# Differential attention between the last tiles of its value product and the first of its output product, with its norms on GpSimd

## The reference, cut to what matters

```python
q = rms_norm(z[..., :1024].reshape(bsz, seq, 8, 2, 64), q_gain)
k = rms_norm(z[..., 1024:2048].reshape(bsz, seq, 8, 2, 64), k_gain)
v = z[..., 2048:].reshape(bsz, seq, 8, 128)
# for each block of 128 queries, 8 heads, 2 halves c of a head:
logits = einsum('bqhcd,bkhcd->bhcqk', q_blk, k) / 8
p = softmax(logits - slope[h] * dist)
attn = p[:, :, 0] - lam * p[:, :, 1]
o = einsum('bhqk,bkhe->bqhe', attn, v)
# after all blocks
o = rms_norm(o, out_gain) * (1.0 - lambda_init)      # over the 128 of a head
x = x + o.reshape(bsz, seq, 1024) @ diff_w_out
```

## Time and profile before

| | us |
|---|---|
| median of 3 executions (1834.36 to 1842.99) | 1838.56 |
| the profiled execution | 1837.14 |
| its span, first to last instruction | 1835.3 |
| TensorE busy | 1746.8 (95%) |
| VectorE, ScalarE, GpSimd busy | 972.2, 766.4, 131.1 |

### The profile page before, as it was taken

The page is one execution under the profiler, slowest core; times in us unless marked ns, Lnnn a source line. Parts: engine busy times, 40 slices in busy tenths (PEclk is TensorE's granted clock), DMA queues, the critical chain, the costliest instruction groups (busy, mean ns, idle before and its releaser), DMA issues.

```text
span 1835.3 us, 32123 instructions
## 1 busy us (share of the span) xinstructions
PE 1746.8 (95%) x14193; PEld 1436.9 (78%) x14193; DVE 972.2 (53%) x1353; ACT 766.4 (42%) x1180; POOL 131.1 (7%) x99
## 2 busy tenths in 40 slices
PE   6998889889999999999999998989999999999999
PEld 5877778778887788888887886558888788888887
DVE  5477656436343465535644345984524355633652
ACT  4243444425553344313433234873654244422430
POOL 1001221230010000000000022010010000000000
PEclk9999999999999999999999999999999999999999
DMA  7210000124331232222222222003322223222321
GB/s 242 81 46 2 4 4 18 48 105 149 114 115 46 73 110 94 92 92 92 92 93 91 95 89 69 1 1 115 115 92 69 92 89 95 92 92 92 92 96 66
DMA packets 96454, 149.42 MB, mean 81 GB/s; under 512 B 3479, under 2 KB 50170, under 8 KB 96314
## 3 DMA queue, kind: packets, MB, share of 16 engines
q1 hardware_dynamic: 94727, 142.29, 23.6%
q0 software_dynamic: 1296, 4.95, 0.8%
q10 hardware_dynamic: 291, 0.12, 0.0%
HBM read 145.25 MB, written 2.10 MB: 80 GB/s over the span
## 4 chain that ended last, share of the span: by engine, by line
PE 85%; DVE 6%; ACT 4%; issue 3%; DMA 1%; POOL 1%; POOLq 0%; SPq 0%; ACTq 0%; DVEq 0%
PE PS L369 69%; PE PS L1023 2%; PE PS L1037 2%; DVE SS L1783 2%; PE PS L548 1%; PE PS L1572 1%; DVE WLO L335 1%; PE PS L1064 1%; PE PS L916 1%; PE PS L1056 1%; PE PS L1541 1%; ACT WHI L329 1%; PE PS L653 1%; PE PS L1696 1%; DMA WRAW<-cross_wq 1%
## 5 line engine op out<-in xcount | busy, mean ns | idle before, releaser
L335 DVE TENSOR_TENSOR WLO<-WRAW,WHI 128x2048 fp32r<-128x2048 f32 (+1 forms) x131 | 294.7, 2251 | 447.5 <-ACT WHI L329 447.5
L329 ACT ACTIVATE WHI<-WRAW 128x2048 fp32r<-128x2048 f32 (+1 forms) x132 | 248.4, 1882 | 421.0 <-PE PS L369 396.9
L369 PE MATMUL PS<-HIS,WHI 128*128 128x512 f32 x856 | 333.8, 390 | 1.5 <-DVE SM L1945 1.5
L369 PE MATMUL PS<-HIS,WLO 128*128 128x512 f32 x856 | 333.0, 389 | 0.0
L369 PE MATMUL PS<-LOS,WHI 128*128 128x512 f32 x856 | 333.0, 389 | 0.0
L369 PE MATMUL PS<-WHI,HIS 128*128 128x512 f32 x608 | 239.1, 393 | 0.0
L369 PE MATMUL PS<-WLO,HIS 128*128 128x512 f32 x608 | 236.8, 389 | 0.0
L369 PE MATMUL PS<-WHI,LOS 128*128 128x512 f32 x608 | 236.7, 389 | 0.0
L369 PEld LDWEIGHTS PS<-HIS,WHI 128*128 128x128 f32 x856 | 160.7, 188 | 35.1 <-DVE SM L1945 1.7
L369 PEld LDWEIGHTS PS<-LOS,WHI 128*128 128x128 f32 x856 | 160.7, 188 | 33.5 <-issue 0.2
L369 PEld LDWEIGHTS PS<-HIS,WLO 128*128 128x128 f32 x856 | 160.7, 188 | 33.4
(11 more groups left out here) (288 smaller groups left out, 2467.3 us busy)
## 6 DMA issues: line engine op xcount, KB each, us to landing
WRAW<-ffn_w_up SPq DMA_DIRECT2D x88, 512.0 KB, 4.5
WRAW<-ffn_w_down SPq DMA_DIRECT2D x20, 1024.0 KB, 5.1
WRAW<-cross_wkv SPq DMA_DIRECT2D x16, 1024.0 KB, 5.1
WRAW<-diff_w_in SPq DMA_DIRECT2D x12, 1024.0 KB, 5.1
WRAW<-ab_w_in SPq DMA_DIRECT2D x10, 1024.0 KB, 5.4
WRAW<-cross_wq SPq DMA_DIRECT2D x8, 1024.0 KB, 5.1
WRAW<-cross_wo SPq DMA_DIRECT2D x8, 1024.0 KB, 5.1
X<-x SPq DMA_DIRECT2D x8, 512.0 KB, 5.0
```

The costliest lines, as they stand in the source:

```text
L329: A.e.activation(part(WHI[place(i)], i), part(WRAW[i % 2], i), ACT.Copy).then_inc(S("w_hi"), 1)
L335: V.e.tensor_tensor(part(WLO[place(i)], i), part(WRAW[i % 2], i), part(WHI[place(i)], i).bitcast(F32), ALU.subtract).then_inc(S("w_lo"), 1)
L369: mm = e.matmul(o, l, r, start=(si == 0 and kk == 0 and q == 0), stop=(si == len(steps) - 1 and kk == nk - 1 and q == 2))
```

## The change

1. All `meet` calls of the stage go.
2. The queries are turned inside the first slab of dv's second group (`turn_amid_pe`: before its banks 2 and 3), so their norm has to be ready there; for that the norm is taken a slab earlier and a tile at a time: four sums beside slab 0, two scalings each beside slabs 1 and 2, and on GpSimd four powers of 16 columns in place of one of 64.
3. The first three attention steps stand between the banks of dv's last slab (`first_steps_pe`); its values are copied by ScalarE inside the loop (`values`).
4. The last three stand between the banks of do's first slab (`last_steps_pe`), whose PSUM banks are 0 to 3.
5. The outputs of heads 0 to 5 are turned in the loop, at the end of steps 11, 15, ... 31 (`dturn_out_pe`, bank 7), head 6 and 7 in and behind do's first slab. PV therefore has one bank (6) and waits for the output copy of the step before.
6. The fused instruction multiplies by -1/8 and takes the minimum, so the scaling L1786 goes, and each exponential waits for its own half only.
7. The squares, sums, variance and scaling of heads 0 to 6 go from VectorE to GpSimd (`dnorm_pool`): a product of 128x512, seven additions of halving width (256, 128, ... 4 columns), a scaling, the power, a product of 128x512, each waiting for the one before. VectorE keeps head 7.
8. SS, AT, ATT, BIAS move in SBUF, since HIS and LOS are still read at the loop's start and written during it.

```diff
     def group_norm_pool(G, tag, nt, w, o=0):
-        n = D // w * nt
-        G.e.wait_ge(*at(tag, "gvar", 1))
-        G.e.tensor_tensor(SM[:, 160 + o:160 + o + n], SM[:, 96 + o:96 + o + n], SM[:, 16:17].to_broadcast([P, n]), ALU.pow)\
-            .then_inc(sem(tag, "grstd"), 1)
+        n = D // w
+        for t in range(nt):
+            c = o + t * n
+            G.e.wait_ge(*at(tag, "gvar", t + 1))
+            G.e.tensor_tensor(SM[:, 160 + c:160 + c + n], SM[:, 96 + c:96 + c + n], SM[:, 16:17].to_broadcast([P, n]),
+                              ALU.pow).then_inc(sem(tag, "grstd"), 1)
...
     def dpv_pe(e, m):
         h, t = divmod(m, NT)
         e.wait_ge(S("datc"), m + 1)
-        if m >= 2:
-
-            e.wait_ge(S("dov"), m - 1)
+        if m:
+            e.wait_ge(S("dov"), m)
...
+    def dturn_out_pe(e, h):
+        e.wait_ge(*at("do", "gn", h + 1))
...
+        for t in range(NT):
+            mm = e.transpose(PS[:, out_bank(h), t * P:t * P + P], OTK[:, t, h * P:h * P + P], ident)
+        mm.then_inc(sem("do", "ttp"), 1)
+
+    def dstep_pe(e, m):
...
+        if m < NM:
+            dlog_pe(e, m)
+        if 2 <= m < NM + 2:
+            dturn_pe(e, m - 2)
+        if m >= 3:
+            dpv_pe(e, m - 3)
+        if OUT_STEP <= m < NM and (m - OUT_STEP) % NT == 0:
+            dturn_out_pe(e, (m - OUT_STEP) // NT)
...
     def dattn_pe(T):
-        for m in range(NM + 3):
...
+        gemm_pe(T, "dv", hhi, hlo, only=[(0, 0), (0, 1)])
+        T.e.wait_ge(*at("dk", "tev", DC))
+        gemm_pe(T, "dv", hhi, hlo, amid=turn_amid_pe(T), only=[(1, 0)])
+        gemm_pe(T, "dv", hhi, hlo, amid=first_steps_pe(T), only=[(1, 1)])
+        for m in range(3, NM):
+            dstep_pe(T.e, m)
+        gemm_pe(T, "do", hhi, hlo, operand=lambda k: at("do", "tev", k), amid=last_steps_pe(T), only=[(0, 0)])
+        dturn_out_pe(T.e, DH - 1)
...
-                e.wait_ge(S("dmx"), m + 1)
                 for c in range(2):
-                    e.activation(SS[m % 3][:, c, :], SS[m % 3][:, c, :], ACT.Exp, scale=DSC, bias=sx(m, 2 + c),
+                    e.wait_ge(S("ds"), 2 * m + c + 1)
+                    e.activation(SS[m % 3][:, c, :], SS[m % 3][:, c, :], ACT.Exp, scale=-1.0, bias=sx(m, c),
                                  accum_out=sx(m, 4 + c)).then_inc(S("de"), 1)
...
+            if h < DH - 1:
+                e.wait_ge(S("dov"), NT * (h + 1))
+                G.mine(e.tensor_tensor(SQP[:, :, :], o, o, ALU.mult))
+                G.wait_mine()
+                for n in (64, 32, 16, 8, 4, 2, 1):
+                    G.mine(e.tensor_tensor(SQP[:, :, 0:n], SQP[:, :, 0:n], SQP[:, :, n:2 * n], ALU.add))
+                    G.wait_mine()
+                G.mine(e.tensor_scalar(v, SQP[:, :, 0], 1.0 / P, EPS, ALU.mult, ALU.add))
+                G.wait_mine()
+            else:
+                e.wait_ge(*at("do", "gvar", 1))
+            e.tensor_tensor(r, v, SM[:, 16:20], ALU.pow).then_inc(sem("do", "grstd"), 1)
+            if h < DH - 1:
+                e.wait_ge(*at("do", "grstd", h + 1))
+                e.tensor_tensor(o, o, r.unsqueeze(2).to_broadcast([P, NT, P]), ALU.mult).then_inc(sem("do", "gn"), 1)
```

More of the change, by code:

```diff
@@ new lines, in out_bank @@
+    def out_bank(h):
+        return 7 if h < DH - 1 else 4
+    def dturn_out_pe(e, h):
+        e.wait_ge(*at("do", "gn", h + 1))
+        if h == 0:
+            e.wait_ge(*at("dv", "ev", 2 * NT))
+        elif h < DH - 1:
+            e.wait_ge(*at("do", "tev", h))
+        for t in range(NT):
+            mm = e.transpose(PS[:, out_bank(h), t * P:t * P + P], OTK[:, t, h * P:h * P + P], ident)
+        mm.then_inc(sem("do", "ttp"), 1)
+    def dstep_pe(e, m):
+        if m == 0:
+            e.wait_ge(*at("dq", "tev", DC))
+        if m < NM:
[6 more added lines that the diff above has]
+            dturn_out_pe(e, (m - OUT_STEP) // NT)
@@ new lines, in turn_amid_pe, with amid, first_steps_pe, last_steps_pe @@
+    def turn_amid_pe(T):
+        def amid(gi, si, b):
+            if b == 2:
+                T.e.wait_ge(*at("dv", "ev", NT))
+                turn_pe(T, "dq", TOKQ, NT, 0, 0, 4)
+            elif b == 3:
+                turn_pe(T, "dq", TOKQ, NT, 0, 4, DC)
+        return amid
+    def first_steps_pe(T):
+        def amid(gi, si, b):
+            if b:
+                dstep_pe(T.e, b - 1)
+        return amid
+    def last_steps_pe(T):
+        def amid(gi, si, b):
+            if b < 3:
+                dstep_pe(T.e, NM + b)
+            if b == 2:
+                dturn_out_pe(T.e, DH - 2)
+            T.e.wait_ge(S("ds"), 2 * NM - 3 + b)
+        return amid
@@ L1769, in dattn_act, with dbias_act, dout_hi_act, dout_lo_dve @@
                 out(m - 3)
+            if OUT_STEP <= m < NM and (m - OUT_STEP) % NT == 0:
+                dout_hi_act(A, (m - OUT_STEP) // NT)
+        dout_hi_act(A, DH - 2)
+        dout_hi_act(A, DH - 1)
+    def dbias_act(A):
+        A.e.wait_ge(S("dist_in"), 16)
+        A.e.activation(BIAS[0][:, :], DIST[:, :], ACT.Copy, scale=-2.0 ** (-8.0 / DH) / DSC).then_inc(S("dbias"), 1)
+    def dout_hi_act(A, h):
+        A.e.wait_ge(*at("do", "ttp", h + 1))
+        A.e.activation(HHI[h][:, :], PS[:, out_bank(h), :], ACT.Copy, scale=SM[:, 27:28]).then_inc(sem("do", "hi"), 1)
+    def dout_lo_dve(V, h):
+        V.e.wait_ge(*at("do", "hi", h + 1))
+        V.e.scalar_tensor_tensor(HLO[h][:, :], PS[:, out_bank(h), :], SM[:, 27:28], HHI[h][:, :].bitcast(F32), ALU.mult,
+                                 ALU.subtract).then_inc(sem("do", "tev"), 1)
     def dattn_dve(V):
@@ L1825, in dattn_dve, with dnorm_pool @@
                 second(m - 1)
-            if m >= 4:
+            if OUT_STEP < m <= NM and (m - 1 - OUT_STEP) % NT == 0:
+                dout_lo_dve(V, (m - 1 - OUT_STEP) // NT)
+            if m >= NM:
                 square(m - 4)
-                if m % NT == 0 and m >= 2 * NT:
-                    normalise(m // NT - 2)
+        dout_lo_dve(V, DH - 2)
         normalise(DH - 1)
-    def dturn_out_pe(T):
-        e = T.e
+        dout_lo_dve(V, DH - 1)
+    def dnorm_pool(G):
+        e = G.e
         for h in range(DH):
[L1837 to L1855, removed]
+            v, r = (SM[:, c + h * NT:c + h * NT + NT] for c in (128, 160))
+            o = OTK[:, :, h * P:h * P + P]
+            if h < DH - 1:
[7 more added lines that the diff above has]
+                G.wait_mine()
+            else:
+                e.wait_ge(*at("do", "gvar", 1))
[3 more added lines that the diff above has]
+                e.tensor_tensor(o, o, r.unsqueeze(2).to_broadcast([P, NT, P]), ALU.mult).then_inc(sem("do", "gn"), 1)
     def load_x(e):
@@ L2227, in pool_program @@
                 group_norm_pool(G, "dq", NT, DHD)
[L2228 to L2233 removed]
+                dnorm_pool(G)
                 G.e.wait_ge(*at("do", "ttp", DC))
```

94 lines of the change are left out of this document (40 added, 54 removed).

## The result

| | before | after |
|---|---|---|
| median of 8 runs each | 1840.9 us | 1827.39 us |
| lowest to highest | 1834.36 to 1844.89 | 1819.98 to 1832.78 |
| ratio | | 0.9922, 95% interval 0.9904 to 0.9939 |
| profiled execution | 1837.14 us | 1826.01 us |
| the stage (defined below) | 171.28 us | 154.72 us |

The changed kernel is faster by 0.8%, 13.5 us by the medians; 1824.5 was forecast.

The account below looks back on a forecast made before the run. TensorE, busy 95% of the span, was taken as the bound: 96.3 + 1.8 + 0.3 + 2.4 + 0.3 = 101.1 us against 114.24, 13.1 less than 1837.14, so 1824.0, given as 1824.5. Own range 1821 to 1828; 8 in 10, 1819 to 1833.

Parts of the forecast that it names:

- The work of TensorE that stays: TensorE from query turn to do: query turns 3.82, 32 steps of 2.74, output turns 4.8, together 96.3 us.
- No separate scaling, exponentials per half: Attention loop: exponentials start 0.61 + 0.19 us sooner and L1786 goes; no gain of its own booked.
- The waits: TensorE's waits: query turn 1.8, filling 0.3, loop 2.4, drain 0.3 us.
- The query turn: In dv's third slab: TensorE waits 1.8 us, between 0 and 3.5, for VectorE's scalings.
- The loop: Attention loop: 0.4 us lost per head (GpSimd's disturbance 0.3, PV 0.1), six heads, 2.4 us.
- T of the drain: After the loop: T of step 32 has no L ahead of it, costing 0.3 us.
- The norms on GpSimd: GpSimd in the loop: a head's norm takes 6 to 12 us, taken 7.5, within 11.6 us per head.
- A: Loop and query turn: GpSimd fits VectorE's gaps, queries in time, no loss; 1819.2, with offset 1820 us; chance 0.13.
- B: Loop: GpSimd's traffic delays AT, each head loses 1.9 us in place of 0.4; 1833 us; chance 0.19.
- C: Loop: GpSimd's chain sets the pace, kernel slower; at 15 us per head 1848 us; chance 0.07.
- D: Query turn and filling: waits at the slabs merely moved, 4 us more, 1829 us; chance 0.09.
- The signs: Trace: head 11.6 to 12.0 us, AT above 1.2 once or twice per head, GpSimd's head 6 to 9, clock 1.00.

Follow-up runs that it names:

- the minimum alone: Kernel before, with only the separate scaling removed (fused instruction takes the minimum, each exponential waits for its own half); stage 163.15 us against 171.28.
- two more products: Changed kernel plus two more 128x512 products on GpSimd per head, results unused; stage 158.77 us against 154.72.
- the norm behind an AT: Changed kernel, but GpSimd starts a head's squares only after VectorE's AT of the next head's third step; stage 156.02 us against 154.72.
- first steps behind the slab: Changed kernel, but attention steps 0 to 2 stand behind dv's last slab, not between its banks; stage 157.40 us against 154.72.

## Why the prediction was right, and where its steps were wrong

The time (1827.39 for 1824.5, inside 1821 to 1828) and the sign were right. The stage gave 16.6 us for 13.1 forecast, and two errors of opposite sign stand in the sum: the work was booked 8.2 us too high, the waits 4.8 too low. That the time fits so well is in part luck. The stage's 3.5 us more are hidden in the profiled execution by the 4.6 us of code that didn't change; the medians' 13.5 us have an interval of 11.2 to 17.7, which holds both 13.1 and 16.6; and 1824.5 adds only 0.5 of the 1.4 us between profiled execution and median that the text names (1825.4 with all of it).

*The work of TensorE that stays: the failed step.* I read 2.74 us per step from the earlier trace rows as work "without an idle gap" and booked 32 of them. The distances after show 2.54; T to PV was 0.60 there and is 0.49, PV to L 1.08 and is 0.99. PV waits for ATT in this step too, but starts at 1167.54 while T's matmuls are shown as running until 1167.60, so TensorE's timeline has no idle time. Its weight loads show the wait; their timeline before, and in the same step with the minimum alone:

```profile
1167.53 0.97 PEld L1713 LDWEIGHTS PS<-VV,ATT 128*128 128x128 f32 x8 [0.17 <-ACT ATT L1739]
```
```profile
1182.52 0.97 PEld L1713 LDWEIGHTS PS<-VV,ATT 128*128 128x128 f32 x8
```

The twenty waits of the matmuls above are those of the other three steps of a head; neither list had been held against these rows. With the turns of outputs at 0.44 (0.60 booked) and of queries at 3.3, the term is 81.3 + 3.5 + 3.3 = 88.1 us, not 96.3.

*No separate scaling, exponentials per half: booked at nothing, worth 8.1 us alone and 10.6 in the changed kernel.* It follows from the same error: against a step of 2.74 VectorE seemed level with TensorE, and ScalarE "is not the bound" since it had idle time. But it was late by its idle time: it waited for the maximum, and PV waited for it. Against 2.54 the 0.8 us by which the exponentials come sooner are on the path.

*The waits: 4.8 booked.* 97.7 us of the stage (114.24 - 16.56) less 88.1 leave 9.6. The query turn was right, place and size (1.54 for 1.8; reached 5.4 us after the slab's start, the scalings done at 7.2, as worked out). The loop loses 0.84 us a head, not 0.4: 4.2 in the five heads from step 11 on and 1.9 in steps 3 to 10, in all 6.1 for 2.4. Its collision came once a head in the step foreseen, but cost nothing where that step has a turn of outputs; what costs is T behind the low part and PV behind the output copy, for which I had 0.1. T of the drain lost 1.2 for 0.3, 0.6 of it from the collision. The rest, 0.8 us, lies in the filling and draining and was not taken apart.

*The norms on GpSimd.* 6.8 us for 7.5 forecast. VectorE without them is worth 3.8 us, in the order tried.

*The rivals.* A (no loss) needs no waits at all, and 9.6 us of them are there; its ground, that VectorE waits for L in most steps, doesn't hold either (9 times in the 28 steps from 1143 to 1228 us before). B: no instruction of the changed kernel costs what it says; two more products made it come true at 0.6 us per head. C: GpSimd has 4.6 us to spare per head. D: no wait was moved; the filling gives 2.7 us and the draining 1.05.

*The signs.* The clock, GpSimd's head and the wait of the query turn came as said. A head took 11.44, under the 11.6 to 12.0 named, as the step of 2.74 was not all work. AT's long ones are 1.03, not above 1.2, and go with the additions, not with the 128x512 rows.

The Trainium skill, GPSIMD Engine Reference, section Key points, named the exposed instructions: those with two SBUF inputs. The trace agrees: AT goes from 0.75 to 1.03, the fused instruction with one input in PSUM keeps its mean of 687 ns in both kernels. That this costs a head in mid-loop no time is a matter of this kernel's slack, which the rule doesn't speak of.

*Open:* with collision and PV's bank both dealt with, a head still takes 11.36 us for 10.60 of TensorE's work. The steps with the low part and the bias are the long ones; which of the two holds the ring was not tried. Nor was a second slot for PV within its bank. What the meetings' removal and the earlier query turn give by themselves was not measured either.

## What to carry to other kernels

Before a step of the bounding engine is taken as work, hold its distances against the shortest ones elsewhere and against the list of waits: a wait of 0.1 to 0.2 us can hide inside pipelined matmuls (the weight loads may show it), and here 0.2 us in each of 32 steps, 6.4 us, had been booked as work. An engine with idle time can still be the one that is late; ask what it waits for and who waits for it, and whether an edit moves that chain forward. And where unchanged code scatters by more than the effect, compare a stage between two fixed events, not times.

## What the runs showed of the hardware

- GpSimd's 128x512 product took 1.04 us here, where rows of the kernel before had 1.28; VectorE's took 0.69. Chained small instructions follow each other after 0.08 us.
- Collisions go both ways: AT took 1.03 beside the additions and 1.55 beside two products; GpSimd's last product took 1.45 in place of 1.04 where AT had started 0.20 us ahead of it (1187.41 and 1187.61, the run with the norm behind an AT). The power of 4 columns beside an AT (1193.82 and 1193.83) left both at their length, 1.02 and 0.75.
- A power of 16 columns took 3.18 us; from 4 and 64 columns I had 2.9.
- With 12.51 us busy of the loop's first 15.7 TensorE's clock stayed at 1.00 (first steps behind the slab); in the kernel before, 12.70 of 15.70 came with 0.89, ahead of them 1.69 us of idle time. No run shows what made the difference.
- Over 324 to 430 us, the same code in all fourteen kernels, the mean granted clock was between 0.90 and 1.00 from one execution to another.
